# Loads moved ahead of three stage starts, and one gating step moved ahead of a remainder, in a two-layer streaming encoder kernel

## The reference, cut to what matters

```python
h = rms_norm(x, norm_g[layer]) * (1 + scale) + shift
qa, ka, va, fa, ga, qb, kb, vb, iq, ik, iw, gb = split_cols(h @ w_in, AB_COLS)
# A: softmax(q k^T / 8 + cum_f[query] - cum_f[key], causal) v     B: softmax over the 256 chosen keys
mixed = concatenate([oa * silu(ga), ob * silu(gb)], axis=-1)
x = x + gate * (mixed @ w_out)          # layer 1: x + gate * ((latent attention) * silu(g)) @ c_w_out
```

## Time and profile before

| | |
|---|---|
| time, median of 3 runs | 1761.96 us (1759.43 to 1762.35) |
| the profiled execution | 1761.5 us, its span 1759.8 us |
| mean granted TensorE clock | 0.971 of full speed |
| PE, DVE, ACT, POOL busy | 93%, 71%, 47%, 12% of the span |
| layer 0's projection ends, attentions start | 632.5 us (last matmul), 636.3 us (first issue of SP) |
| layer 0's attentions end, output projection starts | 938.3 us, 939.6 us |
| layer 1's attention ends, output projection starts | 1634.7 us, 1635.0 us |

### The profile page before, as it was taken

The page is one execution under the profiler, slowest core; times in us unless marked ns, Lnnn a source line. Parts: engine busy times, 40 slices in busy tenths (PEclk is TensorE's granted clock), DMA queues, the critical chain, the costliest instruction groups (busy, mean ns, idle before and its releaser), DMA issues. The chain is left out here.

```text
span 1759.8 us, 34090 instructions
## 1 busy us (share of the span) xinstructions
PE 1637.6 (93%) x12751; PEld 1292.4 (73%) x12822; DVE 1250.1 (71%) x2718; ACT 818.4 (47%) x1815; POOL 218.8 (12%) x297
## 2 busy tenths in 40 slices
PE   4898999999999969989997998999998999999798
PEld 1775677777888857777776887788886787777686
DVE  2777577779989938778887655625536888888764
ACT  3556322211121127778885225523326877777321
POOL 3213000000000022101000000010003223230000
PEclk8899999999999989999998998999999999999899
DMA  9314347652243159998745744324425112111632
GB/s 338 70 43 110 112 111 212 203 168 102 66 133 120 48 145 244 232 230 212 216 152 166 253 155 126 111 87 118 104 73 105 30 31 50 39 31 47 203 127 89
DMA packets 212500, 229.26 MB, mean 130 GB/s; under 512 B 121817, under 2 KB 146497, under 8 KB 211314
## 3 DMA queue, kind: packets, MB, share of 16 engines
q1 hardware_dynamic: 206018, 209.00, 42.5%
q0 software_dynamic: 6320, 18.08, 2.7%
HBM read 169.72 MB, written 54.16 MB: 127 GB/s over the span
## 5 line engine op out<-in xcount | busy, mean ns | idle before, releaser
L907 PE MATMUL PS<-ab_wh,hT 128*128 128x512 f32 x576 | 231.6, 402 | 3.8 <-DVE ab_wl L1304 3.8
L908 PE MATMUL PS<-ab_wl,hT 128*128 128x512 f32 x576 | 226.1, 393 | 0.0
L909 PE MATMUL PS<-ab_wh,hT 128*128 128x512 f32 x576 | 225.5, 392 | 0.0
L1499 DVE TENSOR_SCALAR_CACHE_REDUCE topk_junk<-scores,topk_small 128x528 bf16<-128x528 f32 (+6 forms) x224 | 194.7, 916 | 1.3
L1255 ACT ACTIVATE ab_nat<-PS 128x512 f32<-128x512 f32 x54 | 32.2, 597 | 229.4 <-PE PS L909 229.4
L2747 DVE CUSTOM_DVE_ANT_0 la_S<-PS,la_mask 128x128 f32<-128x128 f32 (+4 forms) x144 | 107.6, 747 | 35.2 <-PE PS L909 31.2
L907 PEld LDWEIGHTS PS<-ab_wh,hT 128*128 128x128 f32 x576 | 108.7, 189 | 31.5 <-issue 5.8
L909 PEld LDWEIGHTS PS<-ab_wh,hT 128*128 128x128 f32 x576 | 108.5, 188 | 24.9
L908 PEld LDWEIGHTS PS<-ab_wl,hT 128*128 128x128 f32 x576 | 108.6, 189 | 21.5
L907 PE MATMUL PS<-out_wh,out_mT 128*128 128x512 f32 x288 | 115.5, 401 | 4.7 <-DVE out_mT L2163 4.7
L1858 ACT ACTIVATE at_P<-at_S,at_nm 128x128 f32<-128x128 f32 (+2 forms) x144 | 110.5, 768 | 17.7 <-DVE at_nm L1903 17.5
(11 more groups left out here) (433 smaller groups left out, 4193.4 us busy)
## 6 DMA issues: line engine op xcount, KB each, us to landing
ab_wl_raw<-in_ab_w_in SPq DMA_DIRECT2D x64, 256.0 KB, 5.3
spare<-in_ada_w SPq DMA_DIRECT2D x32, 512.0 KB, 4.0
out_g<-scratch_gates_nat SPq DMA_DIRECT2D x18, 512.0 KB, 5.5
at_vc<-in_cache_a_v SPq DMA_DIRECT2D x8, 1024.0 KB, 11.2
at_vc<-in_cache_b_v SPq DMA_DIRECT2D x8, 1024.0 KB, 5.3
mod_ada_w<-in_ada_w SPq DMA_DIRECT2D x6, 1024.0 KB, 10.2
c_wl_raw<-in_c_w_in SPq DMA_DIRECT2D x24, 256.0 KB, 5.4
scratch_x1n<-out_x SPq DMA_DIRECT2D x9, 512.0 KB, 2.6
```

Source lines behind the costliest of these rows:

```text
L907: nc.tensor.matmul(out, x[0], w[0], start=start, stop=False)
L908: nc.tensor.matmul(out, x[0], w[1], start=False, stop=False)
L909: return nc.tensor.matmul(out, x[1], w[0], start=False, stop=stop)
L1499: go(V.tensor_scalar(mark, x, limit, 0.0, op, ALU.add, accum_out=cnt[:, m:m + 1]), 0 if m == M - 1 else 1)
```

## The change

Three loads move and one step of DVE changes its place.

- The queries, keys and values of head 0 of branch A load in layer 0's projection: SP does it two steps before the end (`after`, `first_head`), when the stores that these loads read, and the buffers under them, are done. Their tiles get places of their own (`at_q`, `at_k0`, `at_v`), the keys of the three rotating heads become three tensors, and head 0 leaves the loop's loads of `branches_ab`.
- The output weights 2 to 5 of layer 0 load in the attentions, 2 and 3 over the keys' places when head 14 is scored, 4 and 5 over the place of the odd heads' cached keys when those are turned. In layer 1 weights 2 and 3 load over half of the keys' places and weight 4 over a staging tile. `mixed_out` then loads only the rest, behind the gates of token tile 1.
- `gate_rows(2)` goes ahead of `low(1)` in both output projections.

```diff
+def first_head(c, sp):
+    for half in range(2):
+        rows = slice(DH * half, DH * (half + 1))
+        sp.dma_start(c.at_q[rows, 0, :], c.s["qaT"][half, 0:DH, 0:SEQ]).then_inc(store_semaphore("at_head_in0"), 16)
+        for d in range(2):
+            sp.dma_start(c.at_k0[rows, d, :], c.s["kaT"][d, 0:DH, 0:SEQ]).then_inc(store_semaphore("at_head_in0"), 16)
+    values = c.o["p_a_v"][0, 0].rearrange("t h d -> t (h d)")
+    sp.dma_start(c.at_v[:], values[:, 0:2 * DH].rearrange("(j p) n -> p j n", p=P)).then_inc(store_semaphore("at_v_in"), 16)
...
@@ projection, SP
+                if after and s == len(steps) - 2:
+                    sp.wait_ge(mm_done, plan.last(len(groups) - 2) + 1)
+                    for q in range(2):
+                        sp.wait_ge(T_out[q], sent[q])
+                    for q in range(len(steps) - NT - 4, len(steps) - NT):
+                        sp.wait_ge(nat_out[q % 4], stores_until(q))
+                    after(sp)
...
@@ branches_ab, SP
-                for half in range(2):
+                for half in range(2 if g else 0):
...
-                if g == 0:
-                    load_values(0)
...
-            out.fetch_weights(sp)
+            out.fetch_weights(sp, range(2))
             sp.wait_ge(built, 6)
             out.fetch_gates(sp)
+            sp.wait_ge(scored, head_at(G - 2, QT - 1) + 1)
+            out.fetch_weights(sp, range(2, 4))
+            sp.wait_ge(turned, number["keys", G - 1, NP - 1] + 1)
+            out.fetch_weights(sp, range(4, 6))
...
@@ mixed_out, SP
-            for k in range(2, KT):
+            load_gates(1)
+            for k in range(READY, KT):
                 sp.dma_start(raw(k), out.w_dram[k * P:(k + 1) * P, :]).then_inc(w_in[k], 16)
-                if k == 3:
-                    load_gates(1)
             load_x(0)
...
@@ mixed_out, DVE
             for k in range(4, KT):
                 split_low(k)
+            gate_rows(2)
             low(1)
-            gate_rows(2)
...
@@ latent_attention, SP
-            out.fetch_weights(sp)
+            out.fetch_weights(sp, range(2))
             sp.wait_ge(spread, 1)
             out.fetch_gates(sp)
+            sp.wait_ge(scored, head_at(HC - 3, QT - 1) + 1)
+            out.fetch_weights(sp, range(2, 4))
+            sp.wait_ge(expanded, wide_ops(len(wide) - 1))
+            out.fetch_weights(sp, range(4, 5))
```

More of the change, by code:

```diff
@@ L62 @@
 STORES = {}
-STORE_NAMES = [f"{p}_nat_out{n}" for p in ("ix", "ab", "c") for n in range(4)] + ["cum_out", "first_keys", "c_last_out"] + [
-    f"out{l}_{m}{n}" for l in range(2) for n in range(2) for m in ("stored", "row")] + ["out0_w_in0", "out0_w_in1", "out0_g_in0"] + [
+STORE_NAMES = [f"{p}_nat_out{n}" for p in ("ix", "ab", "c") for n in range(4)] + ["cum_out", "first_keys", "c_last_out", "at_head_in0", "at_v_in"] + [
+    f"out{l}_{m}{n}" for l in range(2) for n in range(2) for m in ("stored", "row")] + [f"out0_w_in{k}" for k in range(6)] + ["out0_g_in0"] + [
     f"ab_w_in{k}" for k in range(KT)]
@@ L920, in overlaid, with shared_spots @@
     return raw, stack.enter_context(nc.sbuf_tensor(name, shape, F32R, side=side))
+def shared_spots(nc, stack, name, shape, dt, later, n):
+    with nc.sbuf_tensor(name, shape, dt) as tensor:
+        pass
+    raw, low = overlaid(nc, stack, later, [P, n, D])
+    return tensor, raw, low
 class Front:
@@ L1070, in last, with projection @@
         return max(s for s, (q, i) in enumerate(self.steps) if q == g)
-def projection(nc, c, name, groups, idle=None, side=None, front=None, weights=None, plan=None):
+def projection(nc, c, name, groups, idle=None, side=None, front=None, weights=None, plan=None, after=None):
     S = lambda n: semaphore(nc, f"{name}_{n}")
@@ L1143, in w_loaded, with stores_until @@
             return sum(16 for q in range(g + 1) if k < groups[q].kt)
+        def stores_until(s):
+            total = 0
+            for t in range(s % 4, s + 1, 4):
+                g, i = steps[t]
+                if groups[g].nat:
+                    total += 16 * len(groups[g].nat(i, nat[:, t % 4, :]))
+            return total
         @block.sync
@@ L1752, in score_head @@
                     for d in range(2):
[L1753 removed]
+                        last = nc.tensor.matmul(PS[:, to + a // 512, 0:w], q[:, g % 3, i * P:(i + 1) * P], k[g % 3][:, d, a:a + w],
                                                 start=d == 0, stop=d == 1 and not masked_end)
@@ L1961, in mixed_out @@
     S = lambda n: semaphore(nc, f"out{l}_{n}")
-    w_in, w_hi, w_lo = out.w_in + [S(f"w_in{k}") for k in range(2, KT)], S("w_hi"), S("w_lo")
+    READY = len(out.spots)
+    w_in, w_hi, w_lo = out.w_in + [S(f"w_in{k}") for k in range(READY, KT)], S("w_hi"), S("w_lo")
     g_in, x_in = [out.g_in, S("g_in1")], [S("x_in0"), S("x_in1")]
@@ L2877, in build @@
                 side = Modulation(nc, c, cT, inner)
-                projection(nc, c, "ab", groups, selection(nc, c, [4, 4, 5, 5, 2, 2, 5, 5]), side, weights=weights)
+                projection(nc, c, "ab", groups, selection(nc, c, [4, 4, 5, 5, 2, 2, 5, 5]), side, weights=weights, after=lambda sp: first_head(c, sp))
             retire_semaphores(nc)
@@ L2882, in build @@
             c.mixT = inner.enter_context(nc.sbuf_tensor("mixT", [P, KT, P], F32))
-            out = OutLoads(nc, c, 0, ins["ab_w_out"][0], inner)
+            c.at_k, raw, low = shared_spots(nc, inner, "at_k", [P, 2, 2, SEQ], BF16, "out0_wl23", 2)
+            c.at_kc1, raw2, low2 = shared_spots(nc, inner, "at_kc1", [P, PAST // P, HD], F32, "out0_wl45", 2)
+            spots = [(a[:, n, :], b[:, n, :]) for a, b in ((raw, low), (raw2, low2)) for n in range(2)]
+            out = OutLoads(nc, c, 0, ins["ab_w_out"][0], inner, spots)
             branches_ab(nc, c, out)
@@ L2896, in build @@
             c.mixT = inner.enter_context(nc.sbuf_tensor("mixT1", [P, KT, P], F32))
-            out = OutLoads(nc, c, 1, ins["c_w_out"][0], inner)
+            with nc.sbuf_tensor("la_k", [P, 2, 2, 2, SEQ], BF16) as c.la_k:
+                pass
+            raw, low = overlaid(nc, inner, "out1_wl23", [P, 2, D])
+            inner.enter_context(nc.sbuf_tensor("la_k1", [P, 2, 2, SEQ], BF16))
+            c.la_xs, raw2, low2 = shared_spots(nc, inner, "la_xs", [P, 2, 512], F32, "out1_wl4", 1)
+            spots = [(a[:, n, :], b[:, n, :]) for a, b, m in ((raw, low, 2), (raw2, low2, 1)) for n in range(m)]
+            out = OutLoads(nc, c, 1, ins["c_w_out"][0], inner, spots)
             latent_attention(nc, c, front, out)
```

44 lines of the change are left out of this document (22 added, 22 removed).

## The result

The kernel before took 1762.15 us (median of 4 runs, 1759.43 to 1768.0), the changed kernel 1747.97 us (4 runs, 1745.55 to 1749.09): ratio 0.9905, 95% interval 0.9886 to 0.9925. Three more measurements of the unedited changed kernel gave 0.9923, 0.9912 and 0.9913. So the change is worth about 14.6 us, where 9.6 were forecast.

The account below looks back on a forecast made before the run. The prediction took PE, busy 93% of the span, as the bound, with few long waits on the path; 4.5 + 0.9 + 2.0 + 2.2 = 9.6 us off 1761.5 gave 1751.9 us, range 1747.5 to 1757.5 (about 0.8).

Parts of the forecast that it names:

- Start: Attentions' start: without head 0's loads ahead of it, the first decay is issued and lands earlier; 4.5 us (3.7 to 5.6).
- Value path: Attentions' start: PE no longer waits for POOL's split of head 0's values; 0.9 us (0 to 0.9).
- Output stages: Output projections: PE's second turn no longer waits for gate_rows(2); 2.0 us in layer 0, 2.2 us in layer 1.
- Rival 1: Output projections: gates of tile 2 come no earlier, PE gains nothing there; 1756.1 us, chance 0.11.
- Cost of the moved issues: Projection's end: SP's seven moved issues between gate stores do not delay the block's end; cost 0.
- Heads 1 to 7: Branch A's heads after head 0: the forecast sum held no term for them.
- rival 2: A heads run at their transfers' pace and give the start back; 4.2 us remain, 1757.3 us, chance 0.13.
- rival 3: A heads: PE's stalls grow from instructions arriving late beside full DMA queues; 22.4 us longer, 1774.3 us, chance 0.09.
- rival 4: A heads: stalls shrink as the loads start lighter; half of 13.1 us goes, 1745.3 us, chance 0.09.

Follow-up runs that it names:

- Values late: The changed kernel with head 0's values loaded in the attentions again, behind the decay; ratio to the kernel before 0.9943 (0.9925 to 0.9961).
- values only: The changed kernel with head 0's queries and keys loaded in the attentions again, only its values early; ratio to the kernel before 0.9946 (0.9932 to 0.9960).
- decay part: The changed kernel with the first 384 columns of head 0's decay also loaded in the projection; ratios to the kernel before 0.9920 and 0.9908.
- no start: The changed kernel with head 0's loads put back at the attentions' start; ratio to the kernel before 0.9955 (0.9939 to 0.9972).
- light loads: Kernel before and changed kernel, heads 2 to 7 loading only a quarter of their cached values; ratios to the kernel before 0.9967 and 0.9911.

## Why the prediction was right in its mechanisms and too small

- **Start, 4.5 us forecast.** Right. DVE's wait fell from a mean of 21.0 us (three profiles) to 16.3 (four): 4.8 us. The decay landed 4.1 us after its issue, where 4.9 was taken between bounds of 3.8 and 5.7, so the flight was priced 0.8 us too long. Against the one profile before, the gain is 5.4 us; the mean comes out nearer to the forecast by luck, since DVE waited 0.7 us longer in that profile than in the mean of three. The Trainium skill's fit, DMA: Bandwidth & Descriptors, section Anatomy of one DMA, gave an estimate of 3.2; the trace lies between that and the row of before.
- **Value path, 0.9 us forecast (0 to 0.9). This is the step that failed: its mechanism was right, the term was mis-sized.** It measured 2.5 us in the means (head 0: 20.85 to 18.3). The 0.89 us of PE's wait was priced as idle time alone, and the clock behind it was put at nothing without a reason: PE ran at the lower clock until 8.2 to 9.8 us after the first reduction, and now until 4.0 to 5.3, at half a microsecond of head 0 for each. Values late gives it back, values only keeps it. The upper bound of the term should have held head 0's first matmuls at either clock.
- **Output stages, 2.0 and 2.2 us forecast.** Right: the second turn comes 5.80 - 3.65 = 2.15 us earlier in layer 0, and in layer 1 14.45 us behind the stage's first product instead of 16.67, 2.22. Rival 1 fell; the gates landed in time in both layers, in layer 1 with the small margin foreseen (at 1654.4 on the old scale, as forecast). Neither part of the step does it alone. The bounds were added up loosely: layer 1 had 0 to 2.2 in its own paragraph and 1.2 in the sum, and the upper bounds make 10.7 us, not 11.
- **Cost of the moved issues, 0 forecast.** Right, so far as the profile shows: the gate stores did not hold up the block's end, and the next block's first issue stands 3.72 us behind the projection's last matmul, 3.74 before.
- **Heads 1 to 7, unchanged by forecast.** Right in the mean, but single profiles differ there by up to 6.5 us. Rivals 2, 3 and 4 all lived in these heads; in the profiles none of them came about. The mechanism of rival 3, instructions that come late beside the loads, is there in both kernels, but its sum did not grow. That of rival 2 appears one step further, when the start moves ahead of head 1's keys in decay part.

The stages that the change touches sum to 4.8 + 2.5 + 2.15 + 2.2 = 11.7 us. The spans give the same, 1760.4 in the mean of three profiles before, 1748.7 in four after, 11.7; that they agree so closely is luck, since the projection happened to end 1.7 us later in the four and other stages made up for it. All runs together give 14.6 (means of 98 and of 21 runs, which scatter by 3.1 and 3.6 us). The profiled runs happened to be 1.1 us below the mean of all runs of the kernel before and 1.8 above it for the changed kernel, in the range of that scatter. Whether the remaining 3 us are chance or a gain that these profiles do not show stays open; that no start also gained 3.5 us more in its runs than in its profile speaks against settling it as chance. The forecast had also been made against the one profiled run of 1761.5 us, 1.7 below the mean of 98.

## What to carry to other kernels

A wait of PE in the first microseconds after it has been idle is priced twice: by its own length, and by half of the time by which the rows show PE longer at the lower clock. When a transfer is moved ahead, look for the next transfer in line whose landing does not move: head 1's keys took back a part of what loading some of the decay earlier gave, in one profile most of it. And where one stage varies by several microseconds between profiles of the same kernel, compare the stages that the change touches over several profiles, not the spans of two.

## What the runs showed of the hardware

- A broadcast load of 512 KB took 5.7 us from issue to landing behind the first head's loads, and 4.1 us as the first of its block.
- A microsecond of the first head at a granted clock of 0.50 instead of 1.00 cost half a microsecond: 17.91 us with the clock back after 3.97 us, 18.66 after 5.51.
- A stall of 4.19 us on PE was followed by a clock of 0.50 for some 5 us; the head took 24.04 us, against 17.28 for the same head with light loads.
- All 86 stalls of over 0.4 us without a releaser in heads 1 to 8 of the eighteen profiles ended 2.4 to 3.5 us after the start of a 16 KB packet of an instruction queue.
- Seven equal heads, beside a DMA share of 0.85 to 1.09, took from 126.9 to 133.4 us in four executions of one kernel; with light loads, at 0.72 to 0.90, heads 4 to 7 took 17.2 to 17.3 us each.
